# Expert rows scattered to device memory and read back, with three weight slots of two experts

## The chip, the core and the metric

One NeuronCore of one Trainium2 chip runs the whole program. The metric is the device time of one execution in microseconds. A core has TensorE (matrix products, whose clock is granted at 2.4 or 1.2 GHz), VectorE, ScalarE, GpSimd (POOL) and the queue engine SyncE (SP), on-chip memory of 128 partitions (SBUF), the accumulators that TensorE writes (PSUM), and 16 DMA engines that serve all queues.

## What is computed

Two layers (`DEPTH` = 2) over 512 tokens of width 1024 in float32. Each layer is

```python
u = rms_norm(h, ln1_g[l])
h = h + token_mixer(u, ...)      # four mixers, gates of 4 x 1024 columns, W_branch, W_out
h = h + hier_moe(rms_norm(h, ln2_g[l]), ...)
```

and a last norm follows. `hier_moe` picks for every token one of four groups and in it the best two of eight experts, weights them (`top_w`), and adds for both choices

```python
y = (silu(x @ w1[e]) * (x @ w3[e])) @ w2[e]     # w1, w3: 1024 x 256, w2: 256 x 1024
```

times its weight to the token's row. There are 32 experts, so 1024 (token, choice) rows, and one expert's weights are 3 MB.

## The kernel before

**Stages of a layer.** The norm and the input projection in 23 halves with the mixers between them; the four gates with the branch products (`branch(0)` to `branch(3)`), which leave `merged`; `W_out` in eight halves (`out_half`, c = 0 and 1, t = 0 to 3), beside which the rows are turned (`turn`), the router's logits made (`route`), choices ranked (`rank_start`, `rank_end`) and lists built (`list_tile`); then the experts. `bank_filled` counts the halves: `NH + 32` is the end of the gates, `NH + 36` the end of c = 0 of W_out, `NH + 40` its end.

**Experts.** Expert e and expert e + 16 form pair e; a pair's tile has 64 slots (`CAP`) for each of the two. `toks` holds for slot and pair the token's number, or one that is out of bounds for an empty slot. GpSimd gathers the 128 rows of a pair from `x_dram` into `xg` (an indirect DMA). TensorE turns them (`pair_rows`, L809), ScalarE and VectorE copy them with the gain into `xT`, TensorE makes the up product (`up_product`, 32 instructions on L817, into bank 0), ScalarE the Silu (L1136), VectorE the product `hid` (`gated`, L1668), TensorE turns it (L829), ScalarE copies it to `hT` (L1131), TensorE makes the down product (`down_product`, 16 on L817). ScalarE rounds the result to `yH` (L1143), VectorE subtracts to `yL` (L1671). After two pairs `combine_two` brings the rows back to token order: for each of eight parts of `hs` (128 tokens by 512) four products of the selection matrices `tok_of` (VectorE, L1674) with `yH` and `yL` (L851), and VectorE adds the part to `hs` (L1680). Two banks alternate, so TensorE and VectorE wait for one another there. Eight rounds of 32 products and eight adds make the layer's sum.

**Weights.** `w13` has four places of one expert (w1 and w3, 16 KB per partition), in the memory of `raw` and `ringH`, the slots of the projection weights; `w2` has four of 8 KB. SP issues them in program order: w2 of pair 0 before the last gate, w1 and w3 of pair 0 at `NH + 36`, those of pair 1 and its w2 at `NH + 40`; after that pair i's w1 and w3 when the up product of pair i - 2 is done (`up_filled`) and its w2 when the down product of pair i - 2 is (`down_filled`).

**Around them.** ScalarE packs the residual rows into two buffers `xw` (L1105) and GpSimd stores each to `x_dram` (L1252); all four stores must have landed before the first gather. `choose` and `place` on VectorE lead to `toks` (L1625), which the gather waits for too. Tokens that find no slot of the 64 are handled by `later_windows`, whose loops run zero times where no expert has more than 64. At the start of a layer GpSimd clears `attT`, VectorE's `mask_scores(0)` (L1389) waits for it, and SP stores `hs` to `h_dram`. At its end `first_rows` and `mean_square` of the next layer follow the last adds.

Of the kernel before, what the change touches and what calls it, by code (L numbers as in the profile page):

```python
# [5 lines left out]
L, D, S, P = 2, 1024, 512, 128  # L6
# [5 lines left out]
SUMS = 8 * (NP // 2)  # L12
# [9 lines left out]
PLACE = (0, 2, 1, 3)  # L22
# [39 lines left out]
def trunk(nc, a, out):  # L62
# [7 lines left out]
    def sb(name, shape, dt, off):  # L70
# [3 lines left out]
    x_dram = nc.dram_tensor("x_dram", (S, D), f32, kind="Internal").ap()  # L74


    R_U, R_RAW, R_RH, R_B, R_O, R_T1, R_T2, R_C = (x * KB for x in (0, 32, 64, 96, 112, 144, 176, 198))
# [14 lines left out]
    w13 = sb("w13", [P, 4, 2, 2048], f32, R_RAW)  # L92
    w2 = [sb(f"w2_{x}", [P, 2, D], f32, off) for x, off in
          enumerate((R_B, R_B + 8 * KB, R_T1, R_T1 + 8 * KB))]
# [5 lines left out]
    hTt = [sb(f"hTt{t}", [P, KD, P], f32, R_U + 4 * t * KB) for t in range(NT)]  # L100
    xw = [sb(f"xw{x}", [P, D], f32, R_U + (16 + 4 * x) * KB) for x in range(2)]
    ut = sb("ut", [P, NT, D], f32, R_O + 16 * KB)
    junk2 = sb("junk2", [P, 512], f32, R_U + 24 * KB)
# [31 lines left out]
    rc = sb("rc", [P, 964], f32, R_T2 + 16 * KB)  # L135
    upper, ones, iota, slot_code = rc[:, 0:128], rc[:, 128:256], rc[:, 256:768], rc[:, 768:896]
    group_of, second, tokv = rc[:, 896:928], rc[:, 928:960], rc[:, 960:964]
    wr = sb("wr", [P, KD, NR], f32, R_T2 + 20 * KB)

    xg = [sb(f"xg{x}", [P, D], f32, R_U + 4 * x * KB) for x in range(2)]  # L140
    xT = [sb(f"xT{x}", [P, D], f32, R_U + (8 + 4 * x) * KB) for x in range(2)]
    yH = [sb(f"yH{x}", [P, D], f32r, off) for x, off in enumerate((R_U + 16 * KB, R_O + 12 * KB))]
    yL = [sb(f"yL{x}", [P, D], f32r, off) for x, off in enumerate((R_U + 20 * KB, R_U + 28 * KB))]
    silu = sb("silu", [P, FH], f32, R_U + 24 * KB)
    hid = sb("hid", [P, FH], f32, R_U + 25 * KB)
    hT = sb("hT", [P, 2, P], f32, R_U + 26 * KB)
    tok_of = [sb(f"tok_of{x}", [P, S], f32r, R_O + 2 * x * KB) for x in range(2)]
    tok_w = sb("tok_w", [P, S], f32r, R_O + 16 * KB)
    yHw = sb("yHw", [P, D], f32r, R_O + 4 * KB)
    yLw = sb("yLw", [P, D], f32r, R_O + 8 * KB)  # L150
    slot_of = sb("slot_of", [P, 8, P], f32, R_O + 28 * KB)
# [27 lines left out]
    toks = small("toks", [P, NP], i32); tokf = small("tokf", [P, NP])  # L179
    slot_w = small("slot_w", [P, 2, NP])  # L180
    gi = [small(f"gi{x}", [P, 1], i32) for x in range(2)]
# [5 lines left out]
    rt = [R_T1 + 16 * KB]  # L187
# [14 lines left out]
    eid = rtmp("eid", [P, NT, 2]); code = rtmp("code", [P, 8])  # L202
    pair_of = rtmp("pair_of", [P, 8, NP]); tok_rhs = rtmp("tok_rhs", [P, 8, NP]); w_rhs = rtmp("w_rhs", [P, 8, 2, NP])
    sel = rtmp("sel", [P, NT, 2, NE]); selM = rtmp("selM", [P, NT, NE])
    rk = rtmp("rk", [P, NT, 2, NE])
    assert rt[0] <= R_T1 + 28 * KB and BASE + at[0] <= nc.sbuf_usable_end, (at[0], rt[0])
# [22 lines left out]
    w13_in = [signal(f"w13_in{x}", 32 * 8) for x in range(4)]  # L229
    w2_in = [signal(f"w2_in{x}", 16 * 8) for x in range(4)]  # L230
# [34 lines left out]
    u2_stored = [signal(f"u2_stored{x}", 16 * 2) for x in range(2)]  # L265
# [5 lines left out]
    rows_zeroed = signal("rows_zeroed", 2); lists_ready = signal("lists_ready", 1)  # L271
# [7 lines left out]
    out_high = signal("out_high", NP); out_low_ready = signal("out_low_ready", NP); tokens_ready = signal("tokens_ready", NP)  # L279
# [12 lines left out]
    tmc = lambda t: slice(t * P, (t + 1) * P)  # L292

    block = ctx.enter_context(nc.Block())
    DVE_LINKS, ACT_LINKS, WIN_LINKS = 191, 2, 3
    dve_c = signal("dve_c", DVE_LINKS)
    act_c = signal("act_c", ACT_LINKS)
    index_copied = signal("index_copied", NP - 2)
# [1530 lines left out]
```

## Time and profile before

| | |
|---|---|
| median of 3 runs (1567.91 to 1570.24) | 1568.98 us |
| the profiled execution's own time | 1568.51 us |
| its span, first to last instruction | 1566.7 us |
| mean granted TensorE clock | 0.979 |
| TensorE busy (products / weight loads) | 1475.3 us (94%) / 1030.9 us (66%) |
| VectorE, ScalarE, GpSimd busy | 511.3, 534.1, 479.2 us |
| DMA | 307.33 MB, mean 196 GB/s |
| chain that ended last | TensorE 89%, of it L817 22% and L851 7% of the span |
| products of L851 | 109.0 us with `yH`, 102.6 us with `yL`, 256 each |

The 40 slices of the page show transfers at a share of 0.9 or more only in the two expert stages (slices 14 to 18 and 34 to 38, 367 to 417 GB/s), and below half in most of the rest. A busy TensorE is no proof of a bound, as the ends of products are modelled; the chain of work that ended last says what released what. The stretches to look at are from the end of the gates (about 1200 us in layer 2) to the end of the span; layer 1's lie 771 us earlier.

### The profile page before, as it was taken

The page shows a single profiled execution, that of the slowest core. Times are in us where ns is not written, and L with a number is a line of the kernel's source. Part 1 is how long each engine was busy: PE and PEld are TensorE (multiplying, and loading weights), DVE is VectorE, ACT ScalarE, POOL GpSimd, SP SyncE. Part 2 cuts the span into 40 slices and gives each one's busy share as a digit, 9 for nine tenths or more (in the row PEclk, how much of TensorE's full clock was granted, in tenths as well). Part 3 has the DMA queues.
Part 4 walks back from the last instruction along what each step waited for, and adds up shares of the span by engine and source line. Part 5 has one row for each costly group of instructions (what it writes and reads, how often), then busy time and mean ns, then how long its engine had stood idle before and what let it go on. Part 6 is the DMA issues. An engine that isn't in the chain of part 4 may idle for free.

```text
span 1566.7 us, 20780 instructions
## 1 busy us (share of the span) xinstructions
PE 1475.3 (94%) x7894; PEld 1030.9 (66%) x7894; DVE 511.3 (33%) x1131; ACT 534.1 (34%) x855; POOL 479.2 (31%) x252
## 2 busy tenths in 40 slices
PE   6999999999997899999899999999999979999996
PEld 5888877788886344444488987777888844444443
DVE  3332644301224232333333435442112233233333
ACT  4522576522332212122253336664233322122212
POOL 4534333555632000000154434335567010000000
PEclk9999999999997999999999999999999969999998
DMA  7322222233435899999532222222423369999981
GB/s 255 111 76 81 86 84 67 68 121 134 153 125 215 327 409 387 377 368 392 191 133 86 77 88 68 68 83 86 155 94 131 145 231 417 389 381 388 388 354 55
DMA packets 127364, 307.33 MB, mean 196 GB/s; under 512 B 13576, under 2 KB 87352, under 8 KB 110904
## 3 DMA queue, kind: packets, MB, share of 16 engines
q1 hardware_dynamic: 121528, 293.68, 50.2%
q0 software_dynamic: 5760, 12.59, 2.1%
q8 instruction: 53, 0.87, 0.2%
q14 instruction: 23, 0.19, 0.0%
HBM read 304.15 MB, written 10.49 MB: 201 GB/s over the span
## 4 chain that ended last, share of the span: by engine, by line
PE 89%; ACT 3%; DVE 2%; DMA 2%; issue 2%; POOL 0%; DVEq 0%; SPq 0%; POOLq 0%; ACTq 0%
PE ps L817 22%; PE ps L480 17%; PE ps L481 17%; PE ps L482 17%; PE ps L851 7%; PE ps L646 2%; PE ps L809 1%; PE ps L626 1%; PE ps L634 1%; DMA x_dram<-xw 1%; ACT xT L1122 1%; PE ps L582 1%; PE ps L735 1%; ACT hT L1131 1%; DVE hs L1680 1%
## 5 line engine op out<-in xcount | busy, mean ns | idle before, releaser
L480 PE MATMUL ps<-uH,ringH 128*128 128x512 f32 x720 | 281.9, 392 | 0.0
L481 PE MATMUL ps<-uL,ringH 128*128 128x512 f32 x720 | 280.4, 389 | 0.0
L482 PE MATMUL ps<-uH,ringL 128*128 128x512 f32 x720 | 280.3, 389 | 0.0
L817 PE MATMUL ps<-w,xT 128*64 128x512 f32 x1024 | 229.1, 600 | 2.5 <-ACT xT L1122 2.5
L1186 POOL TENSOR_TENSOR ringL<-raw,ringH 128x2048 fp32r<-128x2048 f32 (+1 forms) x32 | 142.7, 4466 | 144.3 <-ACT ringH L937 144.3
L817 PEld LDWEIGHTS ps<-w,xT 128*64 128x64 f32 x1024 | 74.2, 139 | 151.2 <-issue 148.0
L480 PEld LDWEIGHTS ps<-uH,ringH 128*128 128x128 f32 x720 | 135.2, 188 | 28.9 <-issue 0.7
L482 PEld LDWEIGHTS ps<-uH,ringL 128*128 128x128 f32 x720 | 135.2, 188 | 28.7
L481 PEld LDWEIGHTS ps<-uL,ringH 128*128 128x128 f32 x720 | 135.2, 188 | 27.5
L1233 POOL TENSOR_TENSOR ringL<-raw,ringH 128x2048 fp32r<-128x2048 f32 x32 | 147.0, 4594 | 5.0 <-ACT ringH L1065 5.0
L817 PE MATMUL ps<-w,hT 128*64 128x512 f32 x512 | 116.9, 598 | 19.8 <-ACT hT L1131 19.8
L851 PE MATMUL ps<-yH,tok_of 128*128 128x512 f32 x256 | 109.0, 426 | 16.0 <-DVE hs L1680 10.8
L1271 POOL COPY gi<-toks 128x1 int32 x28 | 5.2, 184 | 374.3 <-PE ps L809 374.3
L1236 POOL TENSOR_TENSOR merged<-merged,term 128x512 f32<-128x512 f32 x48 | 67.0, 1396 | 149.7 <-DVE term L1537 149.7
L1069 ACT ACTIVATE sig<-ps 128x512 f32<-128x512 f32 x64 | 38.3, 598 | 204.1 <-PE ps L482 204.0
L851 PE MATMUL ps<-yL,tok_of 128*128 128x512 f32 x256 | 102.6, 401 | 0.0
L1680 DVE TENSOR_TENSOR hs<-hs,ps 128x512 f32<-128x512 f32 x128 | 86.7, 686 | 39.0 <-PE ps L851 39.0
L480 PE MATMUL ps<-ringH,uH 128*128 128x256 f32 x320 | 94.3, 295 | 3.8 <-POOL ringL L1186 2.5
L1537 DVE TENSOR_TENSOR term<-sig,ps 128x512 f32<-128x512 f32 x48 | 32.9, 686 | 198.4 <-PE ps L482 136.6
L481 PE MATMUL ps<-ringL,uH 128*128 128x256 f32 x320 | 91.9, 287 | 0.0
L482 PE MATMUL ps<-ringH,uL 128*128 128x256 f32 x320 | 91.8, 287 | 0.0
L1671 DVE TENSOR_TENSOR yL<-ps,yH 128x1024 fp32r<-128x1024 f32 x32 | 39.2, 1225 | 151.2 <-ACT yH L1143 151.2
(245 smaller groups left out, 2202.8 us busy)
## 6 DMA issues: line engine op xcount, KB each, us to landing
w<-in_w SPq DMA_DIRECT2D x192, 1024.0 KB, 9.8
raw<-in_w_in SPq DMA_DIRECT2D x54, 1024.0 KB, 5.2
braw<-in_w_branch SPq DMA_DIRECT2D x32, 256.0 KB, 4.4
raw<-in_w_out SPq DMA_DIRECT2D x8, 1024.0 KB, 5.1
h_dram<-hs SPq DMA_DIRECT2D x2, 2048.0 KB, 11.4
hs<-h_dram SPq DMA_DIRECT2D x2, 2048.0 KB, 10.6
x_dram<-xw POOLq DMA_DIRECT2D x8, 512.0 KB, 3.1
hs<-in_x SPq DMA_DIRECT2D x4, 512.0 KB, 9.0
```

Of the source, the lines that this page charges most:

```text
L480: mm(o, h, rh, start=first, stop=False)
L481: mm(o, h, rl_, start=False, stop=False)
L482: return mm(o, l, rh, start=False, stop=last)
L817: ins = mm(o[r], lhs[:, r], rhs[x], start=first, stop=last, skip_group_check=True)
L851: last = mm(bank((1, A[5])[x % 2]), tokens[:, tmc(t)], rows[:, c], start=m == 0, stop=m == len(parts) - 1)
L1069: fn(sig[:, j % 2, :], bank(b), ACT.Sigmoid).then_inc(bank_freed[b].h, 1)
L1186: gp_.tensor_tensor(ringL[:, s, 0:n], raw[:, s, 0:n], ringH[:, s, 0:n].bitcast(f32), ALU.subtract).then_inc(unit_low.h, 1)
L1233: gp_.tensor_tensor(ringL[:, s, :], raw[:, s, :], ringH[:, s, :].bitcast(f32), ALU.subtract).then_inc(unit_low.h, 1)
L1236: gp_.tensor_tensor(merged[:, j, :], merged[:, j, :], term[:, j % 2, :], ALU.add).then_inc(term_added.h, 1)
L1537: v.tensor_tensor(term[:, j % 2, :], sig[:, j % 2, :], bank(A[5]), ALU.mult).then_inc(term_ready.h, 1)
L1671: return v.tensor_tensor(low[:], ps[:, A[0] * 512:A[0] * 512 + 1024], high[:].bitcast(f32), ALU.subtract)
L1680: v.tensor_tensor(o, o, bank((1, A[5])[x % 2]), ALU.add).then_inc(added, 1)
```

## The change

Expert results are no longer combined by products in the loop. GpSimd scatters the rows of pairs 0 to 13 (`NS` = 14) to `y_dram`, at row 2 x token + choice, by the second list in `toks`; empty slots are out of bounds. Before that, at the layer's start, SP clears `y_dram` with four stores of the cleared `attT`, and `mask_scores(0)` waits for them. After pair 13's scatter SP reads `y_dram` back in four parts `yb` of 128 tokens by two choices, and VectorE adds both to `hs` (`sum_rows`), for the first part after the results of pair 14, for the others inside pair 15. Pairs 14 and 15 are still combined by products, in one round of 32. The results of pairs 0 to 13 are copied in halves by ScalarE and VectorE to `yy`.

The weights have three slots of two experts. Slot 0 lies in the memory of `uH` and `uL` and is filled at `NH + 32`, slot 1 at `NH + 36`, slot 2 at `NH + 40` and when `x_dram` is stored; w2 of slot 1 lies where the router's tables are and waits for `plan_kept`, a copy of what later windows need. From pair 3 on pair p is issued after the up and down product of pair p - 3. To make room, tiles move: `xw` is a single buffer, `iota` has 128 columns (so `slot_tokens` is made of four instructions). The loops over pairs are unrolled, and `xg` isn't cleared any more.

```diff
-    w13 = sb("w13", [P, 4, 2, 2048], f32, R_RAW)
+    w13 = [[sb(f"w13_{s}{x}", [P, 2, 2048], f32, off) for x, off in enumerate(offs)] for s, offs in
+           enumerate(((R_U, R_U + 16 * KB), (R_RAW, R_RH), (R_RAW + 16 * KB, R_RH + 16 * KB)))]
...
+                if u == 5:
+                    hold(sp, att_cleared.h, att_cleared.at(lay, 1))
+                    for t in range(NT):
+                        sp.dma_start(y_dram[2 * P * t:2 * P * (t + 1), :].rearrange("(p c) n -> p (c n)", c=2),
+                                     attT[:].rearrange("p h t i -> p (h t i)")).then_inc(y_zeroed.h, 16)
...
+            hold(sp, bank_filled.h, bank_filled.at(lay, NH + 32))
+            w13_fill(0)
             hold(sp, bank_filled.h, bank_filled.at(lay, used_at(U_OUT + 1)))
-            w13_fill(0, 0)
-            w13_fill(0, 1)
+            w13_fill(1)
             hold(sp, bank_filled.h, bank_filled.at(lay, used_at(U_OUT + 3)))
-            w13_fill(0, 2)
-            w13_fill(0, 3)
-            w2_fill(0, 2)
-            w2_fill(0, 3)
-            with sp.Fori(1, NP // 2) as i:
-                for y in range(2):
-                    hold(sp, up_filled.h, up_filled.at(lay, y - 1) + i * 2)
-                    w13_fill(i, 2 * y)
-                    w13_fill(i, 2 * y + 1)
-                    hold(sp, down_filled.h, down_filled.at(lay, y - 1) + i * 2)
-                    w2_fill(i, 2 * y)
-                    w2_fill(i, 2 * y + 1)
+            hold(sp, u2_stored.h, u2_stored.at(lay, 16 * NT))
+            w13_fill(2)
+            w2_fill(2)
+            hold(sp, plan_kept.h, plan_kept.at(lay, 1))
+            w2_fill(1)
+            for p in range(SLOTS, NP):
+                hold(sp, up_filled.h, up_filled.at(lay, p - SLOTS + 1))
+                w13_fill(p)
+                hold(sp, down_filled.h, down_filled.at(lay, p - SLOTS + 1))
+                w2_fill(p)
+
+            hold(sp, down_filled.h, down_filled.at(lay, NS))
+            sp.dma_start(g1[:], a["c_next_gain"][ds(lay, 1), :].partition_broadcast(P)).then_inc(g1_in.h, 16)
+            for x in range(2):
+                hold(sp, y_stored[x].h, y_stored[x].at(lay, 16 * (NS // 2)))
+            for t in range(NT):
+                if t == 2:
+                    hold(sp, up_filled.h, up_filled.at(lay, NS + 1))
+                sp.dma_start(yb[t][:], y_dram[2 * P * t:2 * P * (t + 1), :].rearrange("(p c) n -> p c n", c=2)).then_inc(y_back[t].h, 16)
...
-                if more:
-                    pair_rows(i + y, 1 - y)
-                if behind:
-                    combine_two(i - 1)
-                pe.wait_ge(hidden_ready.h, hidden_ready.at(lay, y + 1) + i * 2)
+                if p + 1 < NP:
+                    pair_rows(p + 1)
+                pe.wait_ge(hidden_ready.h, hidden_ready.at(lay, p + 1))
...
-            for x in range(2):
-                gp_.memset(xg[x][:], 0.0).then_inc(rows_zeroed.h, 1)
...
+            def scatter(p):
+
+                hold(pool, out_high.h, out_high.at(lay, p + 1))
+                hold(pool, out_low_ready.h, out_low_ready.at(lay, p + 1))
+                gp_.indirect_dma_start(y_dram, bass.IndirectOffsetOnAxis(toks[:, 1, p:p + 1], axis=0), yy[p % 2][:], None,
+                                       bounds_check=2 * S - 1, oob_is_err=False).then_inc(y_stored[p % 2].h, 16)
+
             hold(pool, lists_ready.h, lists_ready.at(lay, 1))
-            gather(0, 0)
-            gather(0, 1)
-            with pool.Fori(1, NP // 2) as i:
-                for y in range(2):
-                    gather(i, y)
+            for p in range(3):
+                gather(p)
+            for p in range(NS):
+                if p + 3 < NP:
+                    gather(p + 3)
+                scatter(p)
...
+            def sum_rows(t):
+
+                dve.wait_ge(y_back[t].h, y_back[t].at(lay, 16))
+                link(v.tensor_tensor(hs[:, t, :], hs[:, t, :], yb[t][:, 0, :], ALU.add))
+                v.tensor_tensor(hs[:, t, :], hs[:, t, :], yb[t][:, 1, :], ALU.add).then_inc(rows_summed.h, 1)
+
+            def pair(p):
+                y = p % 2
+                dve.wait_ge(silu_ready.h, silu_ready.at(lay, p + 1))
+                gated(slice(p, p + 1)).then_inc(hidden_ready.h, 1)
+                if p + 1 < NP:
+                    rows_copy(p + 1)
+                if p < NS:
+                    if p >= 2:
+                        dve.wait_ge(y_stored[y].h, y_stored[y].at(lay, 16 * (p // 2)))
+                    dve.wait_ge(down_filled.h, down_filled.at(lay, p + 1))
+                    v.tensor_copy(yy[y][:, 512:1024], bank(A[1])).then_inc(out_low_ready.h, 1)
+                    return
+                if p == NP - 1:
+                    for x in range(2):
+                        last = slot_tokens(tok_of[x], slice(NS + x, NS + x + 1))
+                    last.then_inc(tokens_ready.h, 1)
+                    for t in range(1, NT):
+                        sum_rows(t)
+                dve.wait_ge(out_high.h, out_high.at(lay, p + 1))
                 out_low_rows(yH[y], yL[y]).then_inc(out_low_ready.h, 1)
+                if p == NS:
+                    sum_rows(0)
```

## Rows read from the trace of the kernel before

**Rows 1.** Chain that ended last, in order of time: start us, us, what; layer 2's loop

```profile
1393.26 10.52 PE ps L817 x48
...
1406.31 10.54 PE ps L817 x48
...
1420.60 6.11 PE ps L851 x24
1427.40 10.52 PE ps L817 x48
```

**Rows 2.** Stretches of layer 2 and one store: length, busy times, PEclk, DMA share, GB/s

```profile
789.00:791.00 2.00, 0.70 (x7) 0.49 (x5) 1.51 (x2) 1.86 (x3) 0.21 (x1) 1.00 1.03 412
...
1275.00:1287.00 12.00, 10.65 (x40) 4.21 (x40) 0.69 (x1) 1.14 (x4) 1.20 (x2) 0.69 0.09 27
...
1292.00:1296.00 4.00, 4.00 (x20) 1.29 (x18) 0.32 (x1) 1.02 (x1) 0.00 (x0) 1.00 1.02 425
...
1332.00:1336.00 4.00, 4.00 (x23) 1.48 (x20) 0.00 (x0) 0.29 (x1) 0.00 (x0) 1.00 1.02 407
1336.00:1340.00 4.00, 2.93 (x18) 1.31 (x18) 1.48 (x3) 1.60 (x6) 1.20 (x2) 1.00 0.95 346
...
1352.00:1386.00 34.00, 31.66 (x148) 14.44 (x148) 10.62 (x17) 7.12 (x15) 2.31 (x5) 1.00 0.97 387
...
1520.00:1524.00 4.00, 4.00 (x20) 2.83 (x17) 3.00 (x5) 1.14 (x4) 0.00 (x0) 1.00 1.03 411
1524.00:1528.00 4.00, 4.00 (x18) 2.91 (x18) 2.75 (x4) 0.00 (x0) 0.00 (x0) 1.00 0.09 35
...
1548.00:1552.00 4.00, 4.00 (x13) 3.16 (x12) 1.38 (x2) 0.94 (x1) 0.00 (x0) 0.59 0.01 2
```

**Rows 3.** Timeline, end of layer 2: start, us, engine, line, operation [idle before, releaser]

```profile
1540.23 0.48 DVE L1674 TENSOR_SCALAR tok_of<-rc,tokf 128x512 fp32r<-128x512 f32 x1
...
1541.28 3.65 PE L817 MATMUL ps<-w,hT 128*64 128x512 f32 x16 [0.47 <-ACT hT L1131]
...
1546.04 1.23 DVE L1671 TENSOR_TENSOR yL<-ps,yH 128x1024 fp32r<-128x1024 f32 x1 [5.33 <-ACT yH L1143]
1547.56 0.47 PE L851 MATMUL ps<-yH,tok_of 128*128 128x512 f32 x1 [2.63 <-DVE yL L1671]
```

**Rows 4.** DMA issues: kind, queue, count, KB each, median us to landing

```profile
w<-in_w SPq DMA_DIRECT2D x192, 1024.0 KB, 9.8
...
x_dram<-xw POOLq DMA_DIRECT2D x8, 512.0 KB, 3.1
...
xg<-x_dram,gi POOLq DMA_INDIRECT x28, 8.4
```

**Rows 5.** SP's issues in order of time: start, us of issuing, line, what

```profile
39.97 79.49 SPq L360 DMA_DIRECT2D raw<-in_w_in  x7
...
1197.84 0.37 SPq L360 DMA_DIRECT2D raw<-in_w_out  x1
...
1222.78 34.43 SPq L415 DMA_DIRECT2D w<-in_w  x8
...
1287.72 2.07 SPq L415 DMA_DIRECT2D w<-in_w  x4
```

**Rows 6.** The same chain between W_out and the first pair of layer 2

```profile
1259.96 9.18 DMA x_dram<-xw
1270.24 4.84 DMA xg<-x_dram,toks
1275.12 1.98 PE ps L809 x8
...
1278.32 9.18 PE ps L817 x32
```

**Rows 7.** Timeline of VectorE's choices for the last two tiles, and the list

```profile
1253.07 0.24 DVE L1585 TENSOR_SCALAR off_group<-rc,gf 128x32 f32<-128x32 f32 x1
...
1260.22 2.19 DVE L1585 TENSOR_SCALAR off_group<-rc,gf 128x32 f32<-128x32 f32 x1
1260.52 1.86 POOL L1257 MEMSET xg<- 128x1024 f32 x2
...
1266.87 0.17 DVE L1625 TENSOR_SCALAR toks<-ps 128x16 int32<-128x16 f32 x1 [1.13 <-PE ps L756]
```

**Rows 8.** Timeline of VectorE, first mixer's mask in layer 1

```profile
70.24 2.63 DVE L1389 COPY_PREDICATED attT<-cst,ps 128x512 f32<-128x512 uint32 x4 [5.38 <-PE ps L541]
```

More of the change, by code:

```diff
@@ L133, in trunk @@
     hs = sb("hs", [P, NT, D], f32, R_T2)
[L135 to L151, printed above, removed]
+    rc = sb("rc", [P, 592], f32, R_T2 + 16 * KB)
@@ new lines, in trunk @@
+    upper, ones, iota, slot_code = rc[:, 0:128], rc[:, 128:256], rc[:, 256:384], rc[:, 384:512]
+    group_of, second, entry = rc[:, 512:544], rc[:, 544:576], rc[:, 576:592].rearrange("p (c a) -> p c a", a=2)
+    wr = sb("wr", [P, KD, NR], f32, R_T2 + 18.5 * KB)
+    yy = [sb(f"yy{x}", [P, D], f32, R_O + 4 * x * KB) for x in range(2)]
+    yH = [sb(f"yH{x}", [P, D], f32r, R_O + 4 * x * KB) for x in range(2)]
+    xT = [sb(f"xT{x}", [P, D], f32, R_O + (8 + 4 * x) * KB) for x in range(2)]
+    xg = [sb(f"xg{x}", [P, D], f32, R_O + (16 + 4 * x) * KB) for x in range(2)]
@@ L177, in trunk @@
     den2 = small("den2", [P, 2]); rden = small("rden", [P, 2])
-    toks = small("toks", [P, NP], i32); tokf = small("tokf", [P, NP])
+    toks = small("toks", [P, 2, NP], i32); tokf = small("tokf", [P, NP])
     slot_w = small("slot_w", [P, 2, NP])
-    gi = [small(f"gi{x}", [P, 1], i32) for x in range(2)]
+    gi = small("gi", [P, 1], i32)
+    slot_of = small("slot_of", [P, 8, P])
     wts = small("wts", [P, NT, 2])
@@ L877, in _, with combine_two @@
[L877 to L884 removed]
+            def combine_two():
+                hold(pe, out_low_ready.h, out_low_ready.at(lay, NP))
+                hold(pe, tokens_ready.h, tokens_ready.at(lay, 1))
+                hold(pe, rows_summed.h, rows_summed.at(lay, NT))
+                combine([(tok_of[y], w[y]) for y in range(2) for w in (yH, yL)], (sum_added.h, sum_filled.h), sum_added.at(lay, -1))
@@ L1153, in window_item @@
+            rows_copy(0)
+            act.wait_ge(slot_weights_ready.h, slot_weights_ready.at(lay, 1))
+            for p in range(NP):
+                pair(p)
             def window_item(n, p):
@@ L1551, in _ @@
             branch(2, None)
+            v.memset(wr[:, :, NG:EG], 0.0)
             branch(3, None)
@@ L1673, in slot_tokens @@
             def slot_tokens(to, col):
-                return v.tensor_scalar(to[:], iota, tokf[:, col], None, ALU.is_equal)
+                for t in range(NT):
+                    last = v.tensor_scalar(to[:, tmc(t)], iota, tokf[:, col], -float(t * P), ALU.subtract, ALU.is_equal)
+                return last
             def add_row(x, products, value, added):
@@ L1709, in _ @@
-            pair(0, 1, True, False)
-            with dve.Fori(1, NP // 2 - 1) as i:
-                pair(i, 0, True)
-                pair(i, 1, True, behind=False)
-            pair(NP // 2 - 1, 0, True)
-            pair(NP // 2 - 1, 1, False, behind=False)
+            for p in range(NP):
+                pair(p)
             def window_lists(n):
```

286 lines of the change are left out of this document (135 added, 151 removed).

## Prediction, written before the change was run

> **What bounds the kernel now.** I read the chain of work that ended last first, since it says whose time the span is. In each layer's expert loop it repeats with a period of two pairs of experts: products with the experts' weights, row transposes, and after every second pair the combining products of L851 [rows 1]. From 1393.26 to 1427.40 us that is 34.1 us for two pairs. Of it 1406.31 - 1393.26 = 13.05 us is one pair without combining, and the other pair costs 21.1 us, as 24 to 32 products of L851 with their turns between TensorE and the adds to `hs` lie in it. So the loop is set by TensorE. Then I read the table by stretches for the transfers [rows 2]: in the same loop the 16 DMA engines are busy 0.97 with 387 GB/s. With a full queue they give 425 GB/s at a share of 1.02; the dip to 346 GB/s stands where the queue runs low. The second bound is therefore only a few per cent away, and taking work from TensorE alone cannot gain much per pair. The last weights land at about 1524 us, where the share falls from 1.03 to 0.09 [rows 2], while the final combining begins only at 1547.56 [rows 3]: some 23 us of TensorE work are still behind the last transfer. Layer 1 shows the same picture 771 us earlier, so I work out layer 2 and take it twice.
>
> **Removed: combining in the loop.** Seven of eight rounds of 32 products go, with their 56 adds on VectorE. TensorE then needs 13.05 us per pair, 209 us for 16. On its own that would save 7 x 8 us = 56 us per layer, but the transfers come late next, so this is not the gain.
>
> **Transfers in the loop.** A weight transfer is 1024 KB [rows 4]; a pair of experts has six, 6.29 MB. There are 512 x 2 = 1024 chosen rows of 4 KB over 16 pairs, so a gather moves 64 rows or 0.26 MB on average, and the new scatter as much. A pair costs 6.82 MB. For the rate I take 412 GB/s: bounds are 425 (full queue) and 387 (the loop as it is, including the dips) [rows 2]; I stand near the upper one because a third slot keeps one to two pairs queued, so the dips should go. That a store to device memory costs what a load does is shown by the store of `h_dram`, 412 GB/s at a share of 1.03 [rows 2]. Pace: 6.82 / 0.412 = 16.5 us per pair, against 13.05 us that TensorE needs. The loop becomes bound by transfers.
>
> **When the saturated stretch begins and how much lies in it.** Now the first pair's w1 and w3 are issued at 1222.78, after the first half of W_out, and the next fill for a free slot at 1287.72, when the first pair's up product is over [rows 5]; in between the DMA engines idle (share 0.09 from 1275 to 1287 [rows 2]). After the change slot 0 is filled once the gates are over, which is about 1200 us (the last `out_fill`, with the same condition, is at 1197.84 [rows 5]), slot 1 at 1222.8, both beside W_out, whose own units are queued ahead of them, so at no cost. Slot 2 waits for W_out's end and for `x_dram` to be stored. The fourth store of `x_dram` is issued at 1259.96 and lands 9.18 us later now, beside 6 MB of weights [rows 6]; a store alone lands in 3.1 us (median [rows 4]), and the change puts these weights behind it. So it lands at 1263.1 and weights flow from about 1264.5. From there to the last weight: w1, w3 and w2 of the third pair and w2 of the second (8.4 MB), 13 pairs (81.8 MB), 16 gathers (4.2 MB), 13 scatters (3.4 MB): 97.8 MB, at 412 GB/s 237 us, so the end is at 1501.7. The queue doesn't run dry meanwhile: pair 3 is issued when up product 0 ends (1283.6, below), and the 8.4 MB last until about 1285; afterwards each fill comes 13 us after the last while 16.5 us of transfer are queued. Against 1524 this is 22 us earlier.
>
> **The router's end.** The memsets of `xg` on GpSimd go. Beside them a VectorE instruction of 128x32 took 2.19 us, where it is 0.24 us otherwise [rows 7]; it lies in the chain to the lists, so `toks` is written about 1.9 us earlier than 1266.87 [rows 7], at 1265. As `x_dram` is stored before that, the gather starts near 1265.5 instead of 1270.24. It takes 4.8 us, and from its landing to the first up product are 3.2 us [rows 6]; TensorE's product for the lists' weights, itself 1.9 us earlier, ends at 1271, so the up product starts at 1274.4, 3.9 us earlier, and ends, with the same 9.2 us partly at half clock, at 1283.6. This is not on the path any more; it only feeds the queue in time. If it came 5 us late, the queue would stand still for 3 us.
>
> **The end of the loop.** Transfers run in order, so the last pair's w1 and w3 land 5 us before its w2, at 1496.5; up product to 1503.6. The scatter of pair 13 (down product over at about 1475) should land after some 8.4 us, as loaded gathers do [rows 4], at 1485; the readback is issued at 1485 and 1487 behind the weights still queued. Its four parts of 1.05 MB land at 1504.3, 1506.8, 1509.4 and 1511.9: 4.2 MB that delay no weight. But VectorE has the sum for the first 128 tokens queued ahead of `gated` for pair 15, so it waits for the first part: sum to 1506.8 (two adds of 1024 columns, priced by the 1.23 us of L1671 [rows 3]), `gated` to 1507.4, and ScalarE, TensorE and the last down product wait for that; down product (3.65 us [rows 3]) from 1508.4 to 1512. Without this wait `gated` would run at 1504, so it costs 3 us. VectorE goes on with eight `slot_tokens` of 128 columns (bounded by 0.12 and 0.48 us each, as 512 columns take 0.48 [rows 3]; I take 0.2), six adds (7.4 us) and the low parts (1.23 us): 1517.7. There the final combining begins, against 1547.56: 29.9 us earlier. TensorE idles 6 us before it. Today it idles 2.6 us there and the granted clock falls to 0.59 in the next stretch [rows 2, 3]; a longer one costs perhaps 2 us of half speed. What follows, eight adds and the norm, is unchanged. Gain 28 us per layer.
>
> **Zeroing `y_dram`.** Four stores of 1.05 MB, issued behind unit 5 (39.97 us [rows 5]), 10.3 us at 412 GB/s with the tables ahead of them: over by about 57. The mask that now waits for them runs at 70.24 [rows 8]. SP's next fill comes at about 55 and lands a microsecond later, two units ahead of its use. Cost nothing; were stores half as fast, end 67 and still nothing. Other edits (unrolled loops; the copy of the plan; `wr`'s memset) lie on engines that wait for transfers: nothing. ScalarE and VectorE copy half a result each instead of split and subtract, less than before; GpSimd's scatter stands behind the gather of three pairs later, whose condition is older, so neither blocks.
>
> **Sum.** 2 x 28 = 56 us. The profiled execution took 1568.5 us (span 1566.7 and 1.8 around it), the median is 1569.0: 1512.
>
> **Rivals.**
> (a) The readback or the last scatter comes later, for example as it shares the engines with the weights and lands one part after another behind them; each microsecond counts twice. 8 us per layer gives 1528. For: four parts in series, and three sums on VectorE ahead of the last low parts. Against: issued 16 us before needed.
> (b) The transfers don't get faster than 387 GB/s: 253 us instead of 237, so 32 us less gain: 1544. For: this is what the loop now shows. Against: there TensorE sets the demand, and eleven stretches of 4 us from 1292 on give 407 to 425.
> (c) Slower side: loads and scattered stores in turn cut the rate. The point from which it decides is 97.8 MB / (237 + 28) us = 369 GB/s. At 358 GB/s the stretch takes 273 us, 36 more than forecast, 8 more than now allowed: 2 x 8 = 16 us slower, 1584. Against: a store stretch at 412, gathers in the loop at over 410. The Trainium skill (DMA: Bandwidth & Descriptors, Specifications) gives about 358 GB/s as a core's share of device memory; by this rule the time would be 1584. The trace stands above it nearly everywhere, so it gets little.
> (d) The clock: transfers make TensorE wait some 3.5 us in every pair. If the granted clock fell at each wait and stayed down, a pair would take 24.8 us (11.8 us of products doubled, and 1.2): 117 us more per layer than now, 1803. It decides once more than 3.5 us of products in each pair are doubled; a low stretch like that behind the 2.6 us gap, over before 1552 with its average at 0.59 [rows 2], costs under 2 us and hides in the wait. The Trainium skill (TensorE: Matmul & The Clock Gate, HAM oscillation) tells of a kernel that was throttled again at every wait for data; by it this wait would recur in each pair, which the slack covers.
> (e) The slots don't bring anything, as TensorE still waits for something else (1569).
>
> **How the numbers follow.** Forecast 0.74 (1498 to 1522 by rates of 425 to 405 and by the ends of the small terms), (a) 0.10, (b) 0.08, (c) 0.04, (d) 0.03, (e) 0.01. The range, 1498 to 1536, takes in (a) and the milder half of (b). A measurement tells apart about 0.2%. Faster 0.92, same 0.01, slower 0.07.
>
> **What would show it.** Windows of the loop with a DMA share of 1.00 and over 405 GB/s, with TensorE's idle time put down to the weights; pairs 16.5 us apart from the middle of the loop; the last weights of layer 2 landing at about 1474 (1502 less layer 1's 28 us); `x_dram`'s last store at about 3 us; VectorE's first sum waiting for the readback; final combining 6 us behind the last down product. Wrong if the granted clock leaves 1.00 for most of a pair, if the rate with scatters is under 400 GB/s, or if the mask of the first mixer waits for the zeroing.

## The result, and the profile after

| | before | after |
|---|---|---|
| median of 4 runs | 1569.13 us (1567.91 to 1570.24) | 1526.01 us (1524.82 to 1526.60) |
| ratio | | 0.9724, 95% interval 0.9708 to 0.9741 |
| span of the profiled execution | 1566.7 us | 1524.3 us |
| mean granted TensorE clock | 0.979 | 0.963 |
| bytes moved | 307.33 MB | 331.20 MB |

The change gains 43.1 us, where 57 were forecast. The page's lines on busy time, on what the 40 slices moved and on the chain (shares by engine):

```profile
PE 1392.2 (91%) x7446; PEld 962.1 (63%) x7446; DVE 429.2 (28%) x1022; ACT 506.7 (33%) x843; POOL 498.7 (33%) x248
...
GB/s 237 243 84 84 70 69 70 74 100 159 103 230 141 388 418 416 416 416 417 320 196 135 83 84 76 70 69 70 158 105 157 235 202 390 416 417 417 415 417 125
...
PE 73%; SPq 11%; DMA 8%; DVE 4%; ACT 2%; issue 1%; POOL 0%; DVEq 0%; POOLq 0%; ACTq 0%
```

Both expert stages now stand as plateaus of 415 to 418 GB/s, and the chain, 89% TensorE's before, runs for 19% of the span through SP's queue and through transfers: the loops hang on the weights. Stretches of layer 2 (length, busy times, clock, DMA share, GB/s; to be held against [rows 2]):

```profile
1242.00:1262.00 20.00, 14.69 (x54) 9.59 (x56) 4.48 (x28) 1.45 (x6) 3.18 (x3) 0.53 0.99 394
1262.00:1266.00 4.00, 4.00 (x23) 1.58 (x20) 0.00 (x0) 0.57 (x1) 0.00 (x0) 1.00 0.78 313
1266.00:1270.00 4.00, 2.05 (x12) 0.81 (x12) 1.08 (x2) 2.60 (x7) 0.99 (x1) 1.00 0.85 309
1300.00:1330.00 30.00, 27.86 (x136) 10.12 (x134) 3.73 (x6) 4.98 (x14) 5.08 (x5) 1.00 1.02 416
1360.00:1390.00 30.00, 23.74 (x104) 8.65 (x106) 2.55 (x4) 3.15 (x9) 3.50 (x4) 0.94 1.02 417
1420.00:1450.00 30.00, 23.86 (x104) 8.72 (x102) 3.64 (x6) 4.98 (x14) 3.04 (x3) 0.89 1.02 416
1485.00:1490.00 5.00, 3.68 (x18) 1.20 (x14) 0.00 (x0) 0.47 (x1) 0.00 (x0) 1.00 0.97 401
1490.00:1500.00 10.00, 6.28 (x16) 2.00 (x18) 9.58 (x16) 0.38 (x1) 0.00 (x0) 0.66 0.28 118
```

The rate is 416 to 417 GB/s in the three stretches between 1300 and 1450, with gathers and scatters among the loads; of the pauses of [rows 2] (1275 to 1287, 1336 to 1340) only a dip from 1262 to 1270 is left. And the end of layer 2 in the timeline (start, us, engine, line, what, and in brackets the idle time before it with its releaser), which answers to [rows 3]:

```profile
1449.26 7.09 PE L842 MATMUL ps<-w,xT 128*64 128x512 f32 x32
...
1465.53 8.78 PE L842 MATMUL ps<-w,xT 128*64 128x512 f32 x32 [3.00 <-DMA w<-in_w]
...
1472.68 5.67 SPq L475 DMA_DIRECT2D yb<-y_dram  x4
...
1481.60 7.09 PE L842 MATMUL ps<-w,xT 128*64 128x512 f32 x32 [1.09 <-DMA w<-in_w]
...
1490.32 1.23 DVE L1708 TENSOR_TENSOR hs<-hs,yb 128x1024 f32<-128x1024 f32 x1 [7.43 <-DMA yb<-y_dram]
...
1492.72 0.47 DVE L1685 SCALAR_TENSOR_TENSOR hid<-silu,slot_w,ps 128x256 f32<-128x256 f32 x1
...
1494.41 6.37 PE L842 MATMUL ps<-w,hT 128*64 128x512 f32 x16 [0.47 <-ACT hT L1148]
...
1501.95 1.23 DVE L1688 TENSOR_TENSOR yL<-ps,yH 128x1024 fp32r<-128x1024 f32 x1
...
1503.72 0.77 PE L876 MATMUL ps<-yH,tok_of 128*128 128x512 f32 x1 [2.94 <-DVE yL L1688]
```

The up products of the last three pairs start 16.3 and 16.1 us apart. The last one (1481.60 to 1488.69) is over before VectorE can make `hid` (L1685): VectorE stands in its wait for the first part of the readback until 1490.3, adds it (1490.32, 1491.58), and only then makes `hid`. The chain of waits has the links behind that (start, us, what):

```profile
1464.22 8.37 DMA y_dram<-yy,toks
...
1472.68 17.61 DMA yb<-y_dram
...
1490.32 1.24 DVE hs L1708
1491.58 1.23 DVE hs L1709
```

VectorE has no gap from 1490.32 to the end of `yL` at 1503.2, so the final combining hangs on the readback's first part.

Layer 1's final combining starts at 754.60 us, 21.9 us before the 776.5 of the kernel before. Not all of it is the experts' stage: ScalarE's last sigmoid of the gates, ahead of all that the experts do, is already 1.6 us late in layer 1.

```profile
426.34 0.60 ACT L1069 ACTIVATE sig<-ps 128x512 f32<-128x512 f32 x1 [5.68 <-PE ps L482]
...
1197.78 0.60 ACT L1069 ACTIVATE sig<-ps 128x512 f32<-128x512 f32 x1 [5.68 <-PE ps L482]
```

```profile
427.95 0.60 ACT L1086 ACTIVATE sig<-ps 128x512 f32<-128x512 f32 x1 [5.68 <-PE ps L507]
...
1175.79 0.60 ACT L1086 ACTIVATE sig<-ps 128x512 f32<-128x512 f32 x1 [5.68 <-PE ps L507]
```

(The first two rows are the kernel before, the others the changed one.) From this sigmoid to the final combining, called the stage below, the kernel before takes 350.2 us in layer 1 and 349.8 in layer 2, the changed one 326.7 and 327.9. So the stage gained 23.5 and 21.9 us. Lengths of the stage leave out what an execution won or lost elsewhere, and are given below beside the times.

Times of layer 2 are held against the prediction below with these 21.9 us added, since it was worked out in the clock of before. On that scale the last up product starts at 1503.5 (forecast 1496.5), the readback's first part is there at 1512.2 (forecast 1504.3), and the final combining starts at 1525.6 (forecast 1517.7, before 1547.56).

### The profile page after: what moved, and what is told of

Read it like the earlier page. It is cut to its first block, busy times and chain, and to the rows that moved or that the text cites. A ratio compares the mean times of both kernels' runs of the same rounds, so it can differ in the third digit from the quotient of the medians.

```text
span 1524.3 us, 18860 instructions
## 1 busy us (share of the span) xinstructions
PE 1392.2 (91%) x7446; PEld 962.1 (63%) x7446; DVE 429.2 (28%) x1022; ACT 506.7 (33%) x843; POOL 498.7 (33%) x248
## 2 busy tenths in 40 slices
DMA packets 133713, 331.20 MB, mean 217 GB/s; under 512 B 16085, under 2 KB 89861, under 8 KB 115192
## 4 chain that ended last, share of the span: by engine, by line
PE 73%; SPq 11%; DMA 8%; DVE 4%; ACT 2%; issue 1%; POOL 0%; DVEq 0%; POOLq 0%; ACTq 0%
PE ps L505 18%; PE ps L506 17%; PE ps L507 17%; PE ps L842 10%; SPq L435 8%; DMA w<-in_w 3%; SPq L429 3%; DMA yb<-y_dram 2%; PE ps L671 2%; PE ps L651 1%; PE ps L659 1%; DMA y_dram<-yy,toks 1%; PE ps L607 1%; DMA xg<-x_dram,toks 1%; PE ps L834 1%
## 5 line engine op out<-in xcount | busy, mean ns | idle before, releaser
L842 PE MATMUL ps<-w,xT 128*64 128x512 f32 x1024 | 246.5, 637 | 36.3 <-DMA w<-in_w 33.8
L842 PEld LDWEIGHTS ps<-w,xT 128*64 128x64 f32 x1024 | 83.1, 147 | 196.1 <-issue 192.7
L842 PE MATMUL ps<-w,hT 128*64 128x512 f32 x512 | 121.4, 618 | 30.1 <-ACT hT L1148 30.1
L1279 POOL DMA_INDIRECT xg<-x_dram,toks x32 | 32.8, 1025 | 233.9 <-PE ps L834 216.5
L842 PEld LDWEIGHTS ps<-w,hT 128*64 128x64 f32 x512 | 35.0, 141 | 96.1 <-issue 58.1
L1152 ACT ACTIVATE silu<-ps,slot_w 128x256 f32<-128x256 f32 x32 | 15.2, 474 | 237.6 <-PE ps L842 237.6
L1685 DVE SCALAR_TENSOR_TENSOR hid<-silu,slot_w,ps 128x256 f32<-128x256 f32 x32 | 15.4, 480 | 259.2 <-ACT silu L1152 259.2
L1286 POOL DMA_INDIRECT y_dram<-yy,toks x28 | 28.3, 1010 | 156.8 <-DVE yy L1721 151.5
```

Source lines behind the costliest of these rows:

```text
L842: ins = mm(o[r], lhs[:, r], rhs[x], start=first, stop=last, skip_group_check=True)
L1279: gp_.indirect_dma_start(xg[p % 2][:], None, x_dram, bass.IndirectOffsetOnAxis(toks[:, 0, p:p + 1], axis=0), bounds_check=S - 1, oob_is_er ...
```

## The experiments

All kernels are the changed kernel with an edit. Where a median of five stands, the kernel before ran nine times on the same chip (medians 1569.26 to 1569.75 us). For two_deep it ran seven times (median 1568.68 us). Executions of one kernel lie 2 to 7 us apart here, which is much beside most of the steps. In layer 2 of these kernels the clock reading of an event also holds what came ahead of it.

**What the third slot is worth.** In this kernel the three slots stay, but pair p is issued only when the products of pair p - 2 are over, as with two slots, and pair 2 isn't loaded ahead:

```diff
-            w13_fill(2)
-            w2_fill(2)
...
-            for p in range(SLOTS, NP):
-                hold(sp, up_filled.h, up_filled.at(lay, p - SLOTS + 1))
+            for p in range(2, NP):
+                hold(sp, up_filled.h, up_filled.at(lay, p - 1))
                 w13_fill(p)
-                hold(sp, down_filled.h, down_filled.at(lay, p - SLOTS + 1))
+                hold(sp, down_filled.h, down_filled.at(lay, p - 1))
```

> SP issues the weights of pair p only when the up product of pair p - 2 is over (from pair 2 on), as in the kernel before; the rest is as changed. Theory A (the loop is bound by transfers, and the third slot's gain is that one pair's weights and no pause lie outside the saturated stretch): the transfers pause between about 1253 and 1265 us of layer 2 again and 14 pairs follow, 95 MB at 417 GB/s, so the last weights land 12 us later per layer: 1550 us. Rival B (the gain comes from TensorE's relief alone, the slots are without effect): 1526 us, as the changed kernel.

Measured: 1546.42 us (1545.01 to 1548.42, four runs), ratio 0.9853 (0.9835 to 0.9870). So 20.4 of the 43.1 us are the third slot's, and 22.7 come with the rest of the change, of which the loop without combining is the large part (not tried apart). Stretches of this kernel, two around its first pairs and one of the loop:

```profile
1254.00:1276.00 22.00, 18.05 (x75) 9.93 (x76) 4.86 (x25) 4.32 (x11) 4.16 (x4) 0.69 0.49 172
1276.00:1282.00 6.00, 6.00 (x32) 2.00 (x30) 0.69 (x1) 0.60 (x1) 1.01 (x1) 1.00 1.00 418
1390.00:1430.00 40.00, 33.93 (x146) 12.17 (x142) 3.73 (x6) 4.98 (x14) 4.04 (x4) 0.91 1.02 417
```

In the loop, loads that run two pairs ahead keep the DMA engines as full as three do (417 GB/s). The difference is the start: 172 GB/s from 1254 to 1276, which is 1244 to 1266 on the changed kernel's clock (layer 1 costs this one 10 us more), where the third slot's loads give 394 (1242 to 1262, above). The third slot is a head start of 10 to 11 us per layer (the stage is 10.7 and 11.1 us longer here), not a higher rate.

**What each share of the traffic is worth.** The first kernel lets the scatters find every slot but row 0 out of bounds, the second the gathers too, the third loads only half of w1 and w3 from pair 3 on:

```diff
-                                       bounds_check=2 * S - 1, oob_is_err=False).then_inc(y_stored[p % 2].h, 16)
+                                       bounds_check=0, oob_is_err=False).then_inc(y_stored[p % 2].h, 16)
```

> The scatter's bound is set to row 0, so it writes no expert rows but that of index 0 (the sum then lacks pairs 0 to 13); its issue, its semaphores and the readback stay. Theory A: 3.4 MB per layer leave the saturated stretch, 8 us per layer, 1510 us. Rival B (TensorE with its clock sets the pace): 1526. On the 4 us by which the slowest DMA engine is behind the mean at the loop's end: if rows of half empty lists load the engines unevenly, this halves and the time is 1506; if the engines are uneven of themselves, it stays at 4 us.

> Scatter and gather both move only rows of index 0 (experts compute on stale rows). Theory A: 7.6 MB per layer less, 18 us per layer, a pair every 15.1 us: 1490 us; and 1482 if the engines' unevenness comes from the rows and goes with them, so that the up products start as soon as the mean of the engines has landed the weights. Rival B: 1526.

> From pair 3 on only the first half of w1 and w3 of each expert is loaded (the products use stale values for the rest). A pair's transfers are then 4.7 MB or 11.3 us, less than TensorE's 13.05 us. Theory A: TensorE becomes the bound, pairs come every 13.05 us, the granted clock stays at 1.00 in the loop since the waits go, and the last pair starts 26 us earlier per layer: 1474 us. Rival B: the loop keeps its pace, 1526.

Measured, one run each: 1502.76, 1482.71 and 1466.24 us. The 13 scatters ahead of the last weights are 3.4 MB, 8.2 us at 416 GB/s or 16.4 us for both layers; the time fell by 23.3. The gathered rows are 4.2 MB, 20.2 us for both; it fell by 20.0 more. Together 43.3 us, of which bytes explain 36.6. By the stage alone the two steps are 20.2 and 18.4 us, 4 more and 2 less than the bytes; the rest came outside the stage, and the 4 us are the size by which a lag fell that is taken up below. With half of w1 and w3 the limit becomes TensorE's again:

```profile
1411.15 7.04 PE L846 MATMUL ps<-w,xT 128*64 128x512 f32 x32
...
1424.20 7.04 PE L846 MATMUL ps<-w,xT 128*64 128x512 f32 x32
```

13.05 us per pair and no wait for weights, the pace that [rows 1] promised. Its stretch from 1300 to 1330 still shows a DMA share of 1.02, with 371 GB/s:

```profile
1300.00:1330.00 30.00, 26.80 (x134) 10.25 (x132) 4.90 (x8) 6.87 (x20) 5.07 (x5) 1.00 1.02 371
```

A share near 1 says that packets are outstanding, not that somebody waits for them; what releases TensorE does.

**The early fill of slot 0.** `w13_fill(0)` moved behind the wait for half of W_out, where slot 1's stands:

```diff
-            hold(sp, bank_filled.h, bank_filled.at(lay, NH + 32))
-            w13_fill(0)
             hold(sp, bank_filled.h, bank_filled.at(lay, used_at(U_OUT + 1)))
+            w13_fill(0)
             w13_fill(1)
```

> Slot 0 is filled with slot 1 after the first half of W_out instead of at the gates' end. Theory A: 8.4 MB fit into the 35 us until W_out's end, so nothing changes: 1526 us. Rival (the early fill is part of the gain): up to 10 us per layer slower, 1546.

Measured: 1525.31 us (1522.94 to 1526.79), ratio 0.9717 (0.9704 to 0.9730). That part of the change is worth nothing that can be measured here (stage 326.5 and 327.7 us): slot 0's weights are first used at about 1255 us, after the gather, either way.

**The sums of the readback.** Three orders of the same work: the first part's sum moved behind `gated` of pair 15; in addition two of the four sums moved behind the last low parts, beside the final products; and the same with filler products on TensorE (transposes into an unused bank) before the weights' wait from pair 8 on and before the last `hidden_ready` wait.

```diff
                     last.then_inc(tokens_ready.h, 1)
-                    for t in range(1, NT):
+                    for t in range(2):
                         sum_rows(t)
...
-                if p == NS:
-                    sum_rows(0)
+                if p == NP - 1:
+                    for t in range(2, NT):
+                        sum_rows(t)
```

(this is the second of the three; TensorE's wait for `rows_summed` ahead of the last products goes with it, and the filler is the function below)

```diff
+            def filler(n):
+                for _ in range(n):
+                    nc.tensor.transpose(bank(A[5])[:, 0:P], ident, ident)
...
+                if p >= 8:
+                    filler(20)
                 pe.wait_ge(w13_in[s].h, w13_in[s].at(lay, 64 * (p // SLOTS + 1)))
```

> The sum of the first 128 tokens moves on VectorE from behind pair 14 to pair 15, behind the gated product and the selection matrices. If the wait for the readback ahead of the gated product sets the end: the last down product starts 3.5 us earlier and at full clock, but six sums and the low parts still follow on VectorE, so 1 to 2 us per layer: 1523. If VectorE's queue of sums is the whole of it: 1526.

> As sum0_later, and the low parts of pair 15 come ahead of the sums of tokens 256 to 511, and TensorE doesn't wait for all sums before the final combining. VectorE's work is the same, but the last combining starts some 5 us earlier beside it: 3 us per layer, 1520. If the end is set by VectorE's total work: 1524.

> As sums_split, with 20 idle transposes (2.7 us) on TensorE ahead of the wait for the weights of pairs 8 to 15 and 24 ahead of the last gated product, so that the clock stays up. If the low clock in the waits costs nothing, as the loop is bound by transfers: equal to sums_split within 1 us per layer, with up products of 7.1 instead of 9.5 us. If it costs: 2 us per layer less, 1516.

Measured, in this order: 1523.22 us (1522.83 to 1525.58), ratio 0.9707 (0.9694 to 0.9721); 1520.41 us (1519.92 to 1524.79), ratio 0.9696 (0.9683 to 0.9709); and with filler 1521.42 us (1520.87 to 1527.82), ratio 0.9695 (0.9682 to 0.9709). So 2.8 us for the first sum and 2.8 for the two others. The intervals of single steps overlap, and that of both together touches the changed kernel's; but from the sigmoid of layer 1 on, the profiled executions have 1.8 and 5.5 us less than the changed kernel's, and with the two other slot orders below the same edit gave 5.9 and 7.9 us. The tail can be had back in part by moving adds. With filler the clock of the loop stays up (first row; the changed kernel's row for this stretch shows 0.89) and every late up product takes 7.09 us, the last among them (second row; this profiled execution was the slowest of the five and lost some 7 us between the two stages, so its reading says nothing of when weights land):

```profile
1420.00:1450.00 30.00, 26.88 (x138) 11.02 (x139) 3.06 (x6) 4.40 (x14) 3.04 (x3) 1.00 1.02 416
```

```profile
1484.59 7.09 PE L842 MATMUL ps<-w,xT 128*64 128x512 f32 x32 [0.47 <-DMA w<-in_w]
```

and the time is the same within its spread (ratios 0.9695 and 0.9696; the stage takes 321.6 and 321.8 us with filler, 320.9 and 321.4 without). The falling clock in the waits of the loop is real and free: a product that takes 8.8 us instead of 7.1 only shortens the next wait for weights.

**Why the last up product comes late.** Each transfer raises its semaphore 16 times, as often as there are DMA engines, and the trace has the time of each count; they are read here as one count per engine. For the last pair's fourth load of w1 and w3 the mean of the 16 is about 1476.6 us (an estimate from the 64 counts of four loads 2.5 us apart), the last is 1481.5, and the up product starts at 1481.60. The first part of the readback is a single transfer on its semaphore, so its 16 counts can be read without an estimate: their mean is 1485.6 us, ten of them lie between 1484.2 and 1486.3, and the last four at 1487.6, 1487.8, 1490.1 and 1490.3. So two engines are behind by some 4.5 us and two by 2, and VectorE waits for the last. From the mean to the last count are 4.7 us here (3.8 in layer 1), 2.2 without scattered rows and 1.1 without any rows. In the kernel before, the 16 counts of the last w2 lie within 0.6 us of one another.

Gathers and scatters give an engine the rows of certain partitions, and an empty slot gives next to nothing. An expert has 19 to 42 rows here, and they fill the first of its 64 slots. By the routing of these inputs and the 0.16 us that the packet of a 4 KB row takes in the trace, two rules of how partitions go to engines both lay an excess over the mean on the fullest engine: partition modulo 16 one of 4.4 to 4.7 us, and the rule below one of 6.0 to 6.4 us (156 rows on the fullest engine in layer 2). The Trainium skill (DMA: Bandwidth & Descriptors, The descriptor swizzle) states the second for a transfer to 128 partitions: engine 8 x (p / 64) + ((p / 4) mod 8), each quotient rounded down. Two orders of the slots tell the rules apart, one that fills the second expert's 64 from the end and one that takes the slots of an expert in steps of four partitions (127 rows on the fullest engine of layer 2 by the second rule, 29 x 0.16 = 4.6 us fewer). The part of the line that differs:

```diff
-    np.where(p < CAP, p, 1024 + p - CAP)
+    np.where(p < CAP, p, 1024 + P - 1 - p)                                     # mirrored
+    p // CAP * 1024 + p % CAP // 32 * 32 + p % 4 * 8 + p // 4 % 8              # spread
```

> As the changed kernel, but the slots of the pair's second expert are filled from partition 127 down instead of from 64 up, so that filled rows of both experts lie mirrored. Theory U (a row goes to the engine given by its partition modulo 16; counting the filled rows of both experts with the inputs' routing, the fullest engine has 34 rows of gather and scatter more than the mean in a layer, 5 us at 0.16 us a row; mirrored it has 3 to 8, 0.5 to 1.2 us): the slowest engine's backlog at the loop's end falls from 5 to 1 us, weights and readback are usable 4 us earlier per layer: 1518 us. If engines took blocks of 8 partitions, the backlog would be 20 us both ways and nothing would change; if the engines differ of themselves, nothing changes either: 1526.

> mirrored and sums_split in one. If the two gains add, as one brings the transfers and the other shortens VectorE's and TensorE's work behind them: 1520 less 8, 1512 us. If the order of the sums already hides the backlog: 1520.

> As the changed kernel, but the order in which an expert's 64 slots are filled is another: first a partition of each group of four, then the next of each. Theory V: a transfer of 128 rows gives engines 0 to 7 the partitions below 64 and 8 to 15 those above, in groups of four partitions, 32 apart (the Trainium skill, DMA: Bandwidth & Descriptors, The descriptor swizzle); mirroring the second expert within its 64 partitions changed nothing, as this would have it. By the inputs' routing the fullest engine then has 38 to 40 rows of gather and scatter over the mean per layer in the changed kernel, 6.2 to 6.6 us at 0.165 us a row, and 11 to 13, about 2 us, here. The last up product should start 3 to 4 us earlier per layer: 1519 us. If the unevenness has another cause: 1526.

> spread and sums_split in one: if their gains add, 1513 us; if the engines' unevenness isn't the cause, 1520 as sums_split.

| | as changed | with the sums split |
|---|---|---|
| slots in order | 1526.01 | 1520.41 |
| mirrored | 1526.12 (1524.07 to 1526.67), ratio 0.9718 (0.9705 to 0.9731) | 1520.18 (1519.65 to 1524.39), ratio 0.9698 (0.9684 to 0.9711) |
| spread | 1524.66 (1520.81 to 1525.13), ratio 0.9705 (0.9692 to 0.9718) | 1516.81 (1515.27 to 1521.23), ratio 0.9668 (0.9655 to 0.9682) |

The modulo rule falls: mirroring should have gained 8 us and gained none. The last up products of mirrored and of spread, against 1481.60 above:

```profile
1481.71 7.09 PE L842 MATMUL ps<-w,xT 128*64 128x512 f32 x32 [1.08 <-DMA w<-in_w]
```

```profile
1479.11 7.09 PE L842 MATMUL ps<-w,xT 128*64 128x512 f32 x32 [1.15 <-DMA w<-in_w]
```

7 us were expected of each spread kernel; by the medians 1.4 and 3.6 came, the first of which can't be told from none. The stage says more (us, layer 1 and layer 2 of the profiled executions; the last column has the time from the mean to the last of the 16 counts, for the readback's first part in layer 2):

| | stage as changed | stage, sums split | mean to last count |
|---|---|---|---|
| slots in order | 326.7, 327.9 | 320.9, 321.4 | 4.7 and 4.6 |
| mirrored | 326.9, 327.6 | 320.9, 321.5 | 4.8 and 4.8 |
| spread | 323.2, 324.8 | 318.0, 319.5 | 1.8 and 1.6 |

Spread shortens the stage by 3.4 and 3.1 us, with the sums split by 2.9 and 1.9, where 3 to 4 were expected per layer. Its median hides this: in its profiled execution the sigmoid of layer 1, ahead of any expert row, was 2.9 us later than in the changed kernel's, and its final combining ran at half clock for longer and took 1.2 us more than the 7.47 of the changed kernel.

```profile
430.87 0.60 ACT L1086 ACTIVATE sig<-ps 128x512 f32<-128x512 f32 x1 [5.68 <-PE ps L507]
```

```profile
1501.04 8.69 PE ps L876 x24
```

With the sums split, the last up product, the last that SP's loads release, starts at 1478.10 with slots in order and in spread_split at

```profile
1471.36 8.79 PE L842 MATMUL ps<-w,xT 128*64 128x512 f32 x32 [2.52 <-DMA w<-in_w]
```

That the rows of the indirect transfers make engines lag is shown by the two kernels without rows. For the rule of the Trainium skill there is more than the time: by it two engines have 156 and 152 rows in layer 2, two 134 and 128, and the rest 116 or fewer, which is the pattern of the counts above (two far behind, two half as far), where partition modulo 16 gives 145, 137, 131 and two of 126; mirroring leaves it alone, and spreading brought the lag from 4.7 to 1.8 us. The trace agrees with the rule in kind and doesn't name the engines, so it isn't shown engine by engine, and the size is off: the rows counted say 4.6 us less, 2.9 were measured. The 1.1 us that are left without any rows weren't explained. spread_split is the fastest kernel of this case.

## Why the prediction was right, and where its sum was off

**Bound and pace: right.** The bound was taken to move from TensorE to the transfers, at 16.5 us per pair. It is 16.3: from the up product at 1400.18 to the one at 1481.60 there are 81.4 us for five pairs.

```profile
1400.18 8.78 PE L842 MATMUL ps<-w,xT 128*64 128x512 f32 x32 [3.21 <-DMA w<-in_w]
```

The rate is 416 to 417 where 412 was taken, and a scattered store costs what its bytes cost at that rate, apart from the lag. Rival (b), which held the rate at 387 GB/s, and (c), which needed less than 369, fall, and two_deep refutes (e). The Trainium skill (DMA: Bandwidth & Descriptors, Specifications) gives some 358 GB/s as a core's share; the trace stands 16% above it. The Trainium skill (DMA: Bandwidth & Descriptors, Measured) gives 425 GB/s for a core whose neighbour is idle; the trace comes within some 2% of that, so for this program on one core it was the figure to weigh.

**Start and end of the stretch: right within 2 us.** Its start was forecast at 1264.5. The share is 0.99 over the 20 us from 1242, so it starts near 1264 on the old clock, though the stretches from 1262 to 1270 (0.78 and 0.85) lose 1.5 us where the queue wasn't to run dry. The counts of the last w2 have their mean at 1503.7 on the old clock (an estimate as above), against 1501.7.

**The gather: mis-sized, cheap.** 4.8 us were taken from [rows 6], where the queue was nearly empty. With the weights ahead of it, it is

```profile
1244.10 8.23 DMA xg<-x_dram,toks
...
1255.58 9.79 PE ps L842 x32
```

8.2 us, the value that [rows 4] had for loaded gathers (8.4). The prediction moved the transfers ahead of the gather and kept the duration of the unloaded one. Up product 0 ends at 1265.4, so 1287.3, not 1283.6; the fill that waits for it was issued at 1265.4, inside the two stretches just named.

**The last pair: the step that was off.** "The last pair's w1 and w3 land 5 us before its w2, at 1496.5" took a transfer as landed when its share of the bytes has passed. On the old clock the up product started at 1503.5: 7.0 us late, 2.0 by the mean engine (1476.6 + 21.9 = 1498.5) and 5.0 because TensorE waits for the slowest of the 16. This was in no term and no rival, and the trace of before couldn't show it: there the counts of one transfer lie within 0.6 us.

**The readback: right in kind, 8 us late.** VectorE's wait ahead of `gated` was named and priced at 3 us per layer; it is 3.5 us in the trace (from the end of the Silu at 1489.2 to 1492.7), and sum0_later took 2.8 back over both layers, as VectorE's sums still stood ahead of the end. But the first part was usable at 1512.2, not 1504.3. By the mean engine the weights ended 2.0 us late (1503.7), the next layer's gains (512 KB, `c_next_gain`) stand between them and the readback and were in no sum, so that the first part's mean count is at 1485.6 + 21.9 = 1507.5, 3.2 us late; the other 4.7 us are the slowest engine again. They are 2.2 us without scattered rows and 1.1 without any, so the rows cause most of it here too. The scatter took 8.37 us as forecast (8.4), and that it and the readback were issued late (1494.6 on the old clock, not 1485) did no harm, as the queue held weights until 1503.7. So the outcome is rival (a)'s, and its price (8 us per layer, 1528) was close; its reason, parts in series, was not the one. That the range, which was stretched for (a), holds the result is in part luck.

**The tail.** The forecast's six adds stood where they were put. The last down product ran at half clock (6.37 us instead of 3.65) behind the 5.7 us wait, and even that cost nothing: ScalarE had its result rounded at 1501.9, when VectorE's last sum ended. The 2 us per layer that were set aside for the clock in what follows weren't lost either. The final combining and the last instruction of the norm, before and then after:

```profile
1547.56 7.49 PE ps L851 x24
...
1562.36 1.28 DVE ut L1313
```

```profile
1503.72 7.47 PE ps L876 x24
...
1518.49 1.28 DVE ut L1324
```

The same 14.8 us. But the span ends 20.6 us behind the start of the final combining, where before it was 19.1. The 1.5 us come after the last store of the result has landed (1522.5 us): the program ends 1.85 us later, where before it took 0.3 (from 1566.35), and all changed kernels show 1.85. Why stays open. Rival (d) fell, since filler shows that the waits in the loop, with the clock down to 0.89, cost nothing.

**Free, as forecast.** The first mask of layer 1, which waits for the zeroing, runs 1.6 us later than in [rows 8] (first row), but so does all of layer 1 up to the experts, and in no_scatter_rows, with the same zeroing, it runs at the time of before (second row):

```profile
71.85 2.62 DVE L1400 COPY_PREDICATED attT<-cst,ps 128x512 f32<-128x512 uint32 x4 [5.38 <-PE ps L566]
```

```profile
70.11 2.63 DVE L1400 COPY_PREDICATED attT<-cst,ps 128x512 f32<-128x512 uint32 x4 [5.37 <-PE ps L566]
```

It waits for TensorE, by the same 5.4 us, and not for the stores. The transfer that opens the program took 9.68 us, 1.0 more than before. So the zeroing is free, and the 1.6 us belong to this execution's start: in the profiled executions of the changed kernels the mask runs between 70.1 and 71.9 us.

**In sum**, the stage gained 21.9 us in layer 2 where 29.9 were forecast. VectorE's work from the first part on is as long as forecast (13.4 us in both), so the 8 us are the first part's: 4.7 for the slowest engine, 3.2 for the mean one. In layer 1, where the slowest engine was 3.8 us behind the mean, the stage gained 23.5. Over both layers it is 43.8 us to the final combining (1547.56 - 1503.72) instead of 59.8: 16 us missing, 14.4 of them in the two stages and 1.6 in the late start. The 4 us that were set aside for the clock weren't lost, and 1.5 were at the program's end, so that the span is 42.4 us shorter where 56 were forecast.

## What to carry to other kernels

When a loop turns from engine-bound to transfer-bound, work out two more things than bytes over rate: when the slowest DMA engine is through, and which durations of transfers were read from a queue that the change fills. Put the work that hangs on a long readback last on its engine, since whatever stands behind it in program order inherits its lateness. An indirect transfer with empty slots is as uneven as its list: how slots lie on partitions is worth one experiment. And to judge a step of a few us, compare the length of the stage that it touches, from an event ahead of it, and not the times of whole executions, which differ by as much for other reasons.

## What the runs showed of the hardware that was not expected

- 16 DMA engines held 416 to 417 GB/s for over 150 us with 4 KB rows gathered and scattered among 1 MB loads; 387 before was demand, not a limit.
- The readback's first part was usable 4.7 us after the mean of its 16 counts, 2.2 without scattered rows, 1.1 without rows, and 1.8 with the rows spread over the partitions. Two engines made the lag, two more half of it.
- SP isn't free while much is queued: for four loads it took 1.8 us in the early loop and 10 to 12 us later (start, us of issuing). Nothing behind it was urgent here.

```profile
1279.37 1.77 SPq L435 DMA_DIRECT2D w<-in_w  x4
...
1399.02 11.58 SPq L435 DMA_DIRECT2D w<-in_w  x4
```

- The granted clock fell to 0.89 over 30 us of the loop with waits of 1 to 4 us, and was 1.00 with filler products; neither the fall nor the filler moved the time measurably.
